# One decoder layer on one core: weight loads moved to ScalarE's queue, paired scores for the third head group, sums of squares taken head by head on ScalarE

## What is computed

```python
h = rmsnorm(x); z = h @ w_in          # columns: u, va, q, k, v, gate_a, gate_b
q = rotary(rmsnorm(q.reshape(*lead, 24, 64), g_q), pos)   # each head of 64 by its own mean square
k = rotary(rmsnorm(k.reshape(*lead, 24, 64), g_k), pos)
# three head groups (window, dilation) = (128,1), (512,4), (2048,16), 8 heads each
s = einsum(q, k) / 8; s = where(mask, s, NEG); m = max(s); e = exp(s - m); o = (e @ v) / sum(e)
b = sum over groups of o weighted by the groups' softmax denominators
a = u * (tril(w_s) @ va + b_s)        # chunks of 128
x = x + (sigmoid(gate_a) * (a @ w_oa) + sigmoid(gate_b) * (b @ w_ob)) @ w_o
x = x + relu(rmsnorm(x) @ w_ff1) ** 2 @ w_ff2
x = x + sigmoid(rmsnorm(x) @ w_ple_gate) * (pe @ w_ple_proj)
```

## Time and profile before

| | |
|---|---|
| median of three runs | 1116.49 us (1113.86 to 1116.92) |
| the profiled execution | 1118.78 us, span of its instructions 1117.2 us |
| mean granted TensorE clock | 0.98 of full speed |
| busy: TensorE, VectorE, ScalarE, POOL | 95%, 64%, 39%, 22% |

### The profile page before, as it was taken

One profiled execution on the slowest core, in us unless ns is written; L12 is line 12 of the kernel. 1 busy time (PEld: TensorE's weight loads), 2 busy tenths in 40 slices (PEclk: granted clock), 3 DMA queues, 4 the chain that ended last, 5 costly groups with the idle time before them and its releaser, 6 DMA issues.

```text
span 1117.2 us, 21085 instructions
## 1 busy us (share of the span) xinstructions
PE 1061.9 (95%) x8508; PEld 1045.8 (94%) x8508; DVE 709.4 (64%) x917; ACT 430.3 (39%) x737; POOL 251.3 (22%) x390
## 2 busy tenths in 40 slices
PE   8989889998997899899899999999999999999997
PEld 8989889998997799899899989999999999999996
DVE  5679687997987688798945354444444444435552
ACT  5341555536523554324245453322321331233331
POOL 2441233124420005575600210010010011012300
PEclk9999999999998899899899999999999999999998
DMA  6646445677677646475762235555656546645512
GB/s 192 209 131 234 170 138 188 219 229 208 201 240 220 196 152 212 140 210 150 219 211 95 76 114 174 183 178 191 193 164 194 194 159 203 200 160 171 175 51 81
DMA packets 130703, 196.18 MB, mean 176 GB/s; under 512 B 32080, under 2 KB 108144, under 8 KB 128832
## 3 DMA queue, kind: packets, MB, share of 16 engines
q1 hardware_dynamic: 105680, 122.46, 34.8%
q0 software_dynamic: 10816, 64.36, 18.0%
q10 hardware_dynamic: 14128, 8.26, 2.5%
HBM read 186.07 MB, written 62.00 MB: 222 GB/s over the span
## 4 chain that ended last, share of the span: by engine, by line
PE 60%; DVE 14%; DMA 8%; issue 5%; SPq 5%; POOL 4%; ACT 4%; ACTq 0%; DVEq 0%; POOLq 0%
PE gm L1054 55%; DMA w_raw<-in_w_in 5%; SPq L506 3%; DVE w_lo L1331 3%; POOL kv L1836 2%; DVE kv L1459 2%; DMA out_kvp<-V 1%; POOL st L1878 1%; ACT prob L900 1%; DVE st L1353 1%; DVE kv L1500 1%; DVE fin L1373 1%; ACT w_hi L610 1%; DVE acc L1506 1%; SPq L553 1%
## 5 line engine op out<-in xcount | busy, mean ns | idle before, releaser
L1054 PE MATMUL gm<-h_hi,w_hi 128*128 128x272 f32 x1088 | 229.5, 292 | 3.5 <-issue 1.8
L1054 PE MATMUL gm<-h_hi,w_lo 128*128 128x272 f32 x1088 | 226.5, 290 | 0.0
L1054 PE MATMUL gm<-h_lo,w_hi 128*128 128x272 f32 x1088 | 225.7, 289 | 0.0
L610 ACT CAST w_hi<-w_raw 128x1024 fp32r<-128x1024 f32 x150 | 150.9, 1045 | 186.4 <-PE gm L1054 116.5
L1331 DVE TENSOR_TENSOR w_lo<-w_raw,w_hi 128x1024 fp32r<-128x1024 f32 x150 | 177.9, 1227 | 35.8 <-ACT w_hi L610 33.6
L1030 PE MATMUL gm<-w_hi,h_hi 128*128 128x256 f32 x640 | 187.9, 294 | 6.6 <-issue 5.7
L1031 PE MATMUL gm<-w_hi,h_lo 128*128 128x256 f32 x640 | 181.4, 283 | 0.0
L1032 PE MATMUL gm<-w_lo,h_hi 128*128 128x256 f32 x640 | 180.7, 282 | 0.0
L1054 PEld LDWEIGHTS gm<-h_hi,w_hi 128*128 128x128 f32 x1088 | 172.1, 190 | 4.6 <-issue 3.9
L1054 PEld LDWEIGHTS gm<-h_lo,w_hi 128*128 128x128 f32 x1088 | 172.2, 190 | 0.0
L1054 PEld LDWEIGHTS gm<-h_hi,w_lo 128*128 128x128 f32 x1088 | 171.3, 190 | 0.0
(11 more groups left out here) (264 smaller groups left out, 1488.9 us busy)
## 6 DMA issues: line engine op xcount, KB each, us to landing
w_raw<-in_w_ff SPq DMA_DIRECT2D x64, 512.0 KB, 5.2
out_kvs<-in_cache_kv_w POOLq DMA_DIRECT2D x64, 510.0 KB, 4.2
w_raw<-in_w_in SPq DMA_DIRECT2D x60, 512.0 KB, 6.6
kv<-in_cache_kv_w SPq DMA_DIRECT2D x128, 128.0 KB
kv<-in_cache_kv_w SPq DMA_DIRECT2D x64, 256.0 KB
out_kvs<-in_cache_kv_w POOLq DMA_DIRECT2D x32, 508.0 KB, 4.8
kv<-in_cache_kv_w POOLq DMA_DIRECT2D x128, 64.0 KB, 3.6
w_raw<-in_w_o SPq DMA_DIRECT2D x8, 512.0 KB, 4.3
```

Of the source, the lines that this page charges most:

```text
L610: nc.scalar.copy(w_hi[:, r, hh * 1024:(hh + 1) * 1024], w_raw[:, hh]).then_inc(w_hi_done, 1)
L1054: last = nc.tensor.matmul(gm[:, 2 * b2 + half, 0:HALF], w, x[:, k0 + k, half * HALF:(half + 1) * HALF], start=first, stop=end)
```

## The change

1. **Weights.** Panels 2 to 38 are loaded from ScalarE's queue: at sub 1 of panel p, behind `evacuate(s)`, `load_weights(p + 2)` waits until VectorE has read panel p+1 and issues two DMAs. SP keeps panels 0 and 1 and, from the channel mixer on, all. SP's queue is left with chunks, queries and constants up to there, and its first five chunks are spread over slots 4 to 8.
2. **Split after evacuation.** In natural slots ScalarE does `split_hi` behind `evacuate(s)` and not ahead of it.
3. **Sums of squares.** For q and k units ScalarE takes the square of each head by itself, 64 columns at a time, with the sum as a second result (`square_heads`: 8 instructions in sub 0 and 1, 4 in sub 2). VectorE's `sum_squares` is gone; POOL waits for ScalarE. The sums have four places in `st` in place of two.
4. **Scores.** Pieces 24 to 29 are paired; 30 and 31 stay single, since `gm[:, 3]` belongs to units from 61 on.
5. **Order of chunks.** The string moves chunks towards earlier slots up to slot 53; slot 64 has three in place of one, slots 60 to 63 have four in place of seven. The steps "ds" and "sb" come one slot later.

The core of the diff:

```diff
 def paired(j):
-    return PIECES[j][0] < 2
+    return j < 30
...
-CHUNKS_IN_SLOT = ("000000000002112112101102101102213212102102012101112212"
-                  "002113222110020112010100121222200000000000")
+CHUNKS_IN_SLOT = ("000000000101202202102102102102213122102102102102112111"
+                  "112103121030010112010100120313200000000000")
...
-        if s == KEYS_END[2] + 5:
+        if s == VALUES_END + 1:
             order.append((s, ("ds",)))
-        if s == VALUES_END + 1:
+        if s == VALUES_END + 2:
             order.append((s, ("sb",)))
...
-                if sub == 0 and p + 1 < len(PANELS):
-                    load_panel(p + 1)
+                if s == 0:
+                    load_panel(1)
...
-                    for n in range(RING):
-                        load_chunk(n)
+                if 4 <= s < 4 + RING:
+                    sp.wait_ge(unit_ready, s - 1)
+                    load_chunk(s - 4)
...
+            def load_weights(p):
+
+                for hh in range(2):
+                    act.wait_ge(w_lo_done, 2 * (p - 1) + hh + 1)
+                    nk = 1024 // COLS.get(PANELS[p][0], 256)
+                    act.dma_start(w_raw[:, hh].rearrange("p (k n) -> p k n", k=nk), wview(p, hh)).then_inc(w_landed[hh], 16)
...
+            def square_heads(u, rows, at, src, heads, r):
+
+                n = kqn(u)
+                if n >= 4:
+                    act.wait_ge(fin_ready, n - 3)
+                a, c = root_place(n)
+                for x in range(heads):
+                    last = nc.scalar.activation(sq[rows, r, HD * x:HD * x + HD], src[:, HD * x:HD * x + HD], ACT.Square,
+                                                scale=HD ** -0.5, accum_out=st[at, a, c + x:c + x + 1])
+                last.then_inc(act_sums, 1)
...
-                if sub == 0:
-                    split_hi(p + 1, (p + 1) % 2, panel_end(p - 1) if p >= 1 else None)
+                if sub == 0 and kind not in NATURAL:
+                    split_hi(p + 1, (p + 1) % 2, panel_end(p - 1))
...
                 evacuate(s)
+                if sub == 0 and kind in NATURAL:
+                    split_hi(p + 1, (p + 1) % 2, panel_end(p - 1) if p >= 1 else None)
+                if sub == 1 and p + 2 < P_FF:
+                    load_weights(p + 2)
...
-                if tail:
-                    sum_squares(s - 1)
...
-                    if sub < 2:
-                        sum_squares(s)
                     rotate_heads(s)
```

More of the change, by code:

```diff
@@ L707, in square_samples @@
                 act.wait_ge(unit_out, u + 1)
+                if summed_by_act(u):
+                    square_heads(u, slice(NS, 2 * NS), slice(NS, 2 * NS), z[0:NS, r, 0:256], 4, r)
+                    return
                 nc.scalar.activation(sq[0:NS, r, 0:256], z[0:NS, r, 0:256], ACT.Square,
```

41 lines of the change are left out of this document (24 added, 17 removed).

## The result

The changed kernel takes 1103.21 us (median of 4 runs, 1101.55 to 1108.21) against 1116.4 us (the three runs from above and a fourth): a ratio of 0.9887, 95% interval 0.9859 to 0.9915. It is faster by 13 us, just under half of the 27 us that were forecast. The profiled execution was the longest of the four, 1108.21 us with a span of 1106.6 us, so its rows show a launch 5 us above the median.

The account below looks back on a forecast made before the run. Bound before 600 us by TensorE's waits (35.3 us) and slower clock (17.6 us). Terms -5 (panel starts), -3 (squares), -13 (third group), -1 (chunks), -5 ("ds") sum to -27 us, a median of 1090 us; range 1073 to 1110.

Parts of the forecast that it names:

- What bounds it: Before 600 us: TensorE's waits, 35.3 us, and slower clock, 17.6 us; some 50 us to be had at most.
- of the 5.7 us at panel starts I take 5 away: First matmul of a panel, waiting for `w_lo`: earlier weights would remove 5 of 5.7 us.
- the 114 and 376 cases: ScalarE's waits for panels landing near 114 and 376 us, blamed on place in SP's queue, would go.
- a pair of issues at 0.9 us: Cost on ScalarE of issuing a panel's two loads: 0.9 us each pair, 37 panels, 33 us in all.
- The transfers are the limit, not the queue: Rival: panels land as late from ScalarE; third group keeps 9 of 13 us, panel starts 3 of 5; 1102, chance 0.15.
- Squares, -3 us: Slots 0 to 47: ScalarE at 0.38 us a head, 74 us busier, as long as TensorE; probability waits and clock give 3.
- Pairs and third group, -13 us: Stage 335 to 425: timely weights and paired scores end mask waits of 10.4 us; 20.9 at most, 13 taken.
- The wait for V that was feared: Rival: TensorE waits 5 to 6 us in unit 57, clock falls; 8 of 13 us lost, 1098, chance 0.15.
- Chunks, -1 us: Slots 60 to 64: split for slot 66 on time, mixing delayed; bounds -7 to 4.8 us longer, -1 taken.
- "ds", -5 us: Step one slot later meets ready sample denominators: 3.4 us of waits go, and 1.6 us of clock.
- The signs that the prediction named: No ScalarE weight wait over 3 us, slots 0 to 50; units 20, 42 without 3 us waits; ScalarE some 70 us busier.
- one of those named as wrong: Sign against the forecast: mask waits still there, with weights landing 15 us after their issue.

Follow-up runs that it names:

- e16: Kernel before the change with only GpSimd's cache-window copies spread away from slots where weights are late: 1107.36 us, ratio 0.9909.
- e2: Changed kernel with sums of squares back on VectorE, from one ScalarE square of 512 columns: 1116.13 us, ratio 1.000.
- e11: Changed kernel with weights on SP's queue and split as before, and the third group's scores one by one: 1115.31 us, ratio 0.999.
- e3: Changed kernel with the third group's scores one by one again: 1103.46 us, ratio 0.9888.
- e17: Changed kernel with cache-window copies still further from late weights, 6 in slots 3 to 27, 9 in 61 to 77, 17 in 92 to 108: 1097.21 us.
- e4: Changed kernel with the old string of chunks and the steps "ds" and "sb" in their old slots: 1113.23 us, ratio 0.9964.
- e14: Changed kernel with only the steps "ds" and "sb" back in their old slots: 1107.64 us, ratio 0.9931.
- e13: Changed kernel with the old string of chunks and the third group's scores one by one: 1110.91 us, ratio 0.995.
- e9: Changed kernel with cache-window copies spread away from slots where weights are late and from slots 78 to 91: 1097.99 us, ratio 0.9841.
- e1: Changed kernel with all weights loaded from SP's queue again and split at the start of the slot: 1113.95 us, ratio 0.999.
- e15: Changed kernel with cache-window copies spread, and weights on SP's queue and split as before: 1101.97 us, ratio 0.9863.
- e12: Changed kernel storing another tensor in place of V in 1 KB pieces, second and third group; measures time only: 1101.85 us, ratio 0.9873.
- e7: Changed kernel with SP held in each panel's third slot until ScalarE's weights have landed: 1131.7 us, ratio 1.0159.

## Where the prediction was right and which step failed

Two terms fell short of the 27 us: the weights, whose mechanism failed, and the third group, whose waits had been put down to the wrong cause.

- **What bounds it.** Right: waits behind weights and on ScalarE's order, and all of the change before 600 us (466.9 and 466.4 us behind unit 103).
- **Weights, "of the 5.7 us at panel starts I take 5 away; the 114 and 376 cases go, since their load was late by its place in the queue".** This is the step that failed. The case of 376 went, 12 us sooner in issue. The case of 114 had little of it: both kernels issue that panel at 106.5. The time line of a queue shows 16 chunk DMAs ahead of the load and not when the load could have gone; VectorE's row does, where the last read of `w_raw` ends at 103.5, so the queue cost 3 us there:

```profile
101.12 2.35 DVE L1331 TENSOR_TENSOR w_lo<-w_raw,w_hi 128x1024 fp32r<-128x1024 f32 x2
```

In the changed kernel those 3 us went into the later landing of the panel before it. And the step took for granted that a transfer in a queue of its own travels as before. It travels beside chunks which were behind it until then, 16 to 19 us for the panels of slots 18, 39 and 54, and the panel starts wait 12.1 us in all in place of 5.7, 6 us more where 5 less were forecast. What the part did give is at the start: the end of unit 17 comes at 101.0 to 101.9 us in every trace with the weights on ScalarE's queue, at 103.7 to 105.4 with them on SP's. The step also priced a pair of issues at 0.9 us from the shortest row, which has one of 1.84 too; the 37 pairs held ScalarE for 52 us in place of 33, one of them for 6.9 us.
- **The rival.** "The transfers are the limit, not the queue" gave 1102; measured were 1103.2. It lies near, but not by its working: it let the third group keep 9 of 13 us and the panel starts 3 of 5, and the traces show 6 in the third group, nothing from unit 18 to 53 and 8 behind the third group. The row for it, 16 us for the panel of 335 with nothing before it, got a chance of 0.15 only; that very panel, of slot 57, took 6.7 us in the changed kernel, and it was others that took 16 to 19. So the number is near by luck in part. The Trainium skill's rule cited with it ("DMA: Bandwidth & Descriptors", section "Issuing engines are not separate DMA queues": all issuers share the 16 DMA engines) agrees with e16: there moving copies that GpSimd issues takes 9 us off the kernel before, with every weight in SP's queue, and ScalarE's wait for weights goes from 67.2 to 51.9 us.
- **Squares, -3 us.** The price was wrong, 0.38 us a head against 0.20 for full units, and on the high side of the bounds; 0.48 for sample units was above it. ScalarE's busy time rose by 47 us (430 to 477), not 74. Two panels with pairs take 39.9 us, where 39.6 was forecast, and the waits for probabilities halved. Yet the stretch of slots 18 to 53 gained nothing as a whole, since units 18 and 36 gave it back to late weights: 12.8 and 12.3 us in place of 5.7 and 6.6. Undone, the part costs 12.9 us: in company it is the largest, though what share of that is VectorE's time is open (e2).
- **Pairs and third group, -13 us.** The mechanism was wrong. A row "PE waits for the mask of ScalarE" was read as a lack of a second bank, and it was ScalarE standing for weights (rows at e11): its waits for them in that stage fell from 16.4 us to 4.5 with the change. In e3 the pairs give nothing that can be told, and they lengthen the wait at unit 60 (e17). The stage gained 5.7 us, not 13. The wait for V that was feared is 1.5 us.
- **Chunks, -1 us.** Too low: with everything else in place the string is worth 5.6 to 7.5 us (e4 less e14, e13 less e3), 3.7 of them where three chunks left slots 60 to 63.
- **"ds", -5 us.** Right in size, 4.4 us in e14, where the intervals overlap; but it is a gain of 7.9 us with 5.4 given back behind it.
- **Left out.** The stretch from unit 85 to 103 lost 5.9 us in the changed kernel. It takes both changes: with the weights on ScalarE's queue and "ds" a slot later it takes 93.0 us and more in every trace (93.9 in e3, 94.1 in e9, 96.8 in the changed kernel), with "ds" early on the same queue 91.3 and 91.4 (e4, e14), with the weights on SP's queue and "ds" late 91.9 to 92.7 (e1, e11, e15), and 90.9 in the kernel before. No experiment was made for it alone.

The signs that the prediction named: units 20 and 42 have waits of 0 and 2.4 us, the wait at "ds" is gone, ScalarE is busier by less than said; but the first of them, no wait of ScalarE for weights over 3 us in slots 0 to 50, is broken (7.6 us at 333), and one of those named as wrong came true, weights landing 15 us after their issue (18.8 us; the mask waits named beside it are gone). The measured 1103.2 us lies inside the stated range of 1073 to 1110.

## What to carry to other kernels

A queue that holds a transfer back also holds back what would run beside it: before weights get a queue of their own, look at when their buffer comes free and at what the old queue kept behind them; and first move traffic that nobody waits for, which here was one line and gave 5 to 12 us by the medians. A wait that names an engine is a symptom until that engine's own time line has been read: ScalarE wrote the masks late because it had stood for weights. And parts of a change that serve one chain don't add: undone one by one they cost 34 us, together they gave 13.

## What the runs showed of the hardware

- Squares with a sum straight out of the bank overlap down to 0.20 us per head of 128x64 (two instructions); out of `z` in SBUF, 32x64, they take 0.48 us and don't overlap. The smaller one is the slower; whether by its source or its 32 rows was not taken apart.
- The issue of a transfer can hold its engine: a pair of loads took 6.92 us on ScalarE at 221.62, with stores of V before it in the same queue, and 3.68 at 319.56, where a pair took 1.11 at 106.46 and 1.42 at 87.78. The second load of the pair at 221.62 took 6.2 us of that, and 0.7 in e12, with stores in pieces of 1 KB in place of 256 bytes.
- In one queue, 16 chunk DMAs right behind a panel left its second half 6.9 us from issue to landing (e1); from two queues it was 12.9 to 16.1 us (changed kernel, e3, e14), and 5.0 with no chunks issued beside it (e7).
- 512 KB landed after 3.7 us at best and after 21.6 at worst, both in e2 within 30 us. Runs of one kernel spread as well, the four of the changed kernel from 1101.6 to 1108.2 us; that the one makes the other was not shown.
